# Five norms let the next stage's first pair of blocks start on unnormalised rows; masked key halves are left out

## The reference

```python
# first block, l = 0 (even) and 1 (odd)
x = x + even_mixer(rmsnorm(x, norm_mix[0]), ...)      # "f": gmlp gate and causal attention with forgetting
x = x + odd_mixer(rmsnorm(x, norm_mix[1]), ...)       # "o": differential attention and short convolution
x = x + memory_cross_attention(rmsnorm(x, norm_mem_q[l]), rmsnorm(mem, norm_mem_kv[l]), ...)   # "m0", "m1"
h = rmsnorm(x, norm_ffn[l]); x = x + swiglu(h, ...)   # l = 0: "ffn0";  l = 1: a mixture of 8 experts
# second block, l = 0, 1
sh1, sc1, g1, sh2, sc2, g2 = split(silu(c) @ ada_w[l] + ada_b[l], 6)
x = x + g1 * hybrid_mixer(rms_norm(x, norm1_w[l]) * (1 + sc1) + sh1, ...)      # "b0", "b1"
x = x + g2 * conv_ffn(rms_norm(x, norm2_w[l]) * (1 + sc2) + sh2, ...)          # "ffn1", "ffn2"
```

## Time and profile before

| | us |
|---|---|
| runs of the kernel before | 2389.85, 2386.93, 2387.54 |
| median | 2387.54 |
| profiled execution | 2386.44 |
| its span from the first to the last instruction | 2384.6 |
| mean granted clock of TensorE | 0.993 |

### The profile page before, as it was taken

How to read it: one execution, slowest core, us unless ns; L and a number is a source line. 1 busy time by engine, 2 the same in 40 slices (tenths; PEclk the granted TensorE clock), 3 DMA queues, 4 the chain that set the end, 5 groups by cost and what they waited for, 6 DMA issues and landing times.

```text
span 2384.6 us, 39695 instructions
## 1 busy us (share of the span) xinstructions
PE 2341.5 (98%) x14994; PEld 2125.4 (89%) x14994; DVE 1949.3 (82%) x2674; ACT 1522.7 (64%) x2078; POOL 0.8 (0%) x6
## 2 busy tenths in 40 slices
PE   8999999999999999999999999999999999999998
PEld 7999999899978888888888888887999999999998
DVE  6756877986689999999998989897887877886664
ACT  5655443545477887878787878786645554645552
POOL 0000000000000000000000000000000000000000
PEclk9999999999999999999999999999999999999999
DMA  9443779546579898999999999997323658323440
GB/s 378 154 165 142 283 289 350 236 158 267 203 260 375 336 373 338 371 345 362 347 362 346 364 351 360 358 354 306 142 106 142 247 220 329 143 107 141 181 156 19
DMA packets 88271, 623.67 MB, mean 262 GB/s; under 512 B 9764, under 2 KB 11464, under 8 KB 13384
## 3 DMA queue, kind: packets, MB, share of 16 engines
q1 hardware_dynamic: 87600, 621.26, 68.3%
q10 hardware_dynamic: 536, 0.53, 0.1%
HBM read 620.70 MB, written 1.05 MB: 261 GB/s over the span
## 4 chain that ended last, share of the span: by engine, by line
PE 90%; DVE 7%; ACT 2%; issue 1%; DMA 0%; SPq 0%; DVEq 0%; ACTq 0%
PE bank L654 14%; PE bank L656 14%; PE bank L655 14%; PE bank L674 10%; PE bank L678 10%; PE bank L675 10%; PE bank L875 3%; PE bank L874 3%; PE bank L872 3%; DVE ring_r L1745 2%; PE bank L1076 1%; PE bank L1087 1%; PE bank L1244 1%; DVE ring L1730 1%; PE bank L983 1%
## 5 line engine op out<-in xcount | busy, mean ns | idle before, releaser
L1745 DVE TENSOR_TENSOR ring_r<-ring,ring_r 128x1024 fp32r<-128x1024 f32 x402 | 489.5, 1222 | 182.0 <-ACT ring_r L1321 181.5
L1321 ACT ACTIVATE ring_r<-ring 128x1024 fp32r<-128x1024 f32 x402 | 423.0, 1055 | 299.6 <-PE bank L678 134.2
L674 PE MATMUL bank<-XH,ring_r 128*128 128x256 f32 x2000 | 493.0, 284 | 1.9 <-DVE ring_r L1745 1.9
L675 PE MATMUL bank<-XH,ring_r 128*128 128x256 f32 x2000 | 490.5, 283 | 0.0
L2213 DVE TENSOR_TENSOR ring_r<-ring,Z_r 128x1024 fp32r<-128x1024 f32 x336 | 408.4, 1224 | 34.8
L2213 DVE TENSOR_TENSOR ring_r<-ring,mhat_r 128x1024 fp32r<-128x1024 f32 x336 | 402.6, 1221 | 29.9 <-ACT mhat_r L1575 20.5
L1575 ACT ACTIVATE Z_r<-ring 128x1024 fp32r<-128x1024 f32 x336 | 356.7, 1062 | 92.0 <-PE bank L656 91.1
L1575 ACT ACTIVATE mhat_r<-ring 128x1024 fp32r<-128x1024 f32 x336 | 355.6, 1063 | 82.8 <-PE bank L656 81.0
L674 PEld LDWEIGHTS bank<-XH,ring_r 128*128 128x128 f32 x2000 | 383.7, 192 | 3.2 <-DVE ring_r L1745 2.7
L675 PEld LDWEIGHTS bank<-XH,ring_r 128*128 128x128 f32 x2000 | 383.8, 192 | 0.1
L655 PE MATMUL bank<-ring_r,xn_r 128*128 128x512 f32 x896 | 350.2, 391 | 0.0
(11 more groups left out here) (358 smaller groups left out, 3727.9 us busy)
## 6 DMA issues: line engine op xcount, KB each, us to landing
ring<-in_experts SPq DMA_DIRECT2D x336, 1024.0 KB, 6.9
ring<-in_stream SPq DMA_DIRECT2D x245, 1024.0 KB, 7.2
ring<-in_stream SPq DMA_DIRECT2D x8, 512.0 KB, 6.1
xT<-in_xT SPq DMA_DIRECT2D x2, 512.0 KB, 4.6
mhat<-in_memT SPq DMA_DIRECT2D x1, 1024.0 KB, 16.4
swap<-in_early SPq DMA_DIRECT2D x1, 1024.0 KB, 18.3
swap<-in_late SPq DMA_DIRECT2D x1, 1024.0 KB, 10.2
out_T<-xn SPq DMA_DIRECT2D x8, 128.0 KB, 2.0
```

Source lines behind the costliest of these rows:

```text
L674: pe.matmul(dst, hi[:, a], x_hi(kb), start=(n == 0), stop=False)
L675: pe.matmul(dst, lo[:, a], x_hi(kb), start=False, stop=False)
L1321: act.activation(wh(Q), raw(Q), ACT.Copy).then_inc(sems["whi"], 1)
L1745: dve.tensor_tensor(raw(Q, ring_r), raw(Q), wh(Q).bitcast(F32), ALU.subtract).then_inc(sems["wlo"], 1)
```

## The change

For norms 3, 4, 9, 10 and 11 (PLAIN):

- ACT writes x times the gain, unnormalised, as the high part (plain_high), DVE its low part (plain_low), in the residual loop before. PE runs the next stage's first pair of blocks from these (plain_blocks); norm_sums stands inside that pair after tile 5 (6 in norms 4 and 10) of the high products, norm_spread after tile 1 of the low ones. The filler is gone.
- All squares are added up on DVE (direct(i) is 0).
- ACT copies the spread values from PSUM to `roots` in SBUF. DVE multiplies from there, and also scales the first pair's results (scaled). With a shift, two further columns go with the first pair's rows, which give the shift's part of the result; it is added afterwards.
- The second pair, and all that follows, uses the normalised rows as before.
- low() calls are put in other places: after norm_column in each norm; in the o section three calls with rows=False, then low(1), low(2) in place of low(2, rows=False), low(4); modulation_done(0) comes behind o.k's copies; modulation_done(1) and the gain of norm 10 come before ffn1's residual loop.
- ACT's order at norm 10: prep(2) before the root; the evacuations of b1.hf 2 and 3, the shifts of 0 and 1, prep(2), and then the chain on z.

For the attentions f and o (CAUSAL): scores, bias adds, maxima, exponentials, transposes and products with v leave out the wholly masked half of the first query tile (seen, seen_rows); in f the score's four products have 128 columns for the first query tile.

```diff
-EXPOSED = (3, 4, 9, 10, 11)
...
 def direct(i):
-    return 2 if i in (4, 10, 12) else 1
+    return 0 if i in PLAIN else 2 if i == 12 else 1
...
+def plain_blocks(i, dsts, ws, one_bank=False):
+    n, width = PLAIN[i], S + 2 if i in SHIFT else S
+    def sums_between(kb):
+        if kb == (6 if i in (4, 10) else 5):
+            norm_sums(i)
+    def spread_between(kb):
+        if kb == 1:
+            norm_spread(i)
+    return two_blocks(dsts, ws,
+                      lambda kb: plain_hi[:, kb, 0:width], lambda kb: plain_lo[:, kb, 0:width],
+                      lambda kb: W(pe, "uh", n, kb + 1), lambda kb: W(pe, "ul", n, kb + 1), one_bank, sums_between, spread_between)
...
+def root_rows(i):
+    key = f"spread{i}"
+    G.wait_full(act, key)
+    G.drained(act.activation(roots, bank[G.bank(key)][:, 0:S], ACT.Copy), key)
...
 # ACT, a feed-forward stage
+    for kb in range(4, KB):
+        if 4 <= kb < 7:
+            prep()
+        squares(ni, kbs=[kb])
+        plain_high(ni, kb)
+    prep()
     root(ni)
+    root_rows(ni)
     split_x(ni, base)
-    prep()
...
 # DVE, a feed-forward stage
-    norm(ni)
+    norm_column(ni)
+    low(rows=False)
+    norm_apply(ni)
...
+    scaled(first_rows[:, 1, :], ni, f"ffn{i}.gu0", 0, 0 if i else S).then_inc(sems["fr"], 1)
     x_low(inst, base)
-    low(rows=False)
...
 # DVE, the o section
-norm(4)
-x_low("o")
-low(2, rows=False)
-dve.memset(BM[:, :, 0, P:S], NEG)
-low(4)
-modulation_done(0)
+low(1, rows=False)
+norm_column(4)
+low(1, rows=False)
+norm_apply(4)
+x_low("o", kbs=range(0, 4))
+low(1, rows=False)
+x_low("o", kbs=range(4, 8))
+for h in range(2):
+    G.wait_full(dve, "o.q", h)
+for h in range(2):
+    G.drained(scaled(fm(zs(0))[:, h, :], 4, "o.q", h, scale=float(CHUNK) ** -0.5), "o.q", h)
+low(1)
+low(2)
 for h in range(H):
     evac("o.k", h, fm(zs(1))[:, h, :])
     low()
+modulation_done(0)
...
 # ACT, b1
+for m in (2, 3):
+    evac("b1.hf", m, z[:, m * S:(m + 1) * S])
+for m in range(2):
+    W(act, "hz", 0, m + 1)
+    G.drained(act.activation(z[:, m * S:(m + 1) * S], z[:, m * S:(m + 1) * S], ACT.Identity,
+                             bias=shifts[:, 2 + m:3 + m]), "b1.hf", m)
+prep(2)
...
 # PE, f section
+n = (t + 1) * P
+dst = seen(b[:, t * S:(t + 1) * S], t)
+pe.matmul(dst, q4[:, h, t * P:(t + 1) * P], k4[:, h, 0:n], start=True, stop=False)
```

More of the change, by code:

```diff
@@ L395, in build @@
                     release.append((f"{nm[:4]}.res", 3))
+                elif nm in ("ffn1.gu", "ffn2.gu") and j == 0 and q == 0:
+                    release.append((f"{nm[:4]}.g0", 0))
                 elif nm.endswith(".gu") and q % 2:
@@ L424, in plan_mem, with plan_ffn @@
                 G.at[f"m{l}.k", 4 + n] = G.at[f"m{l}.k4", n]
[L426 to L429, removed]
+        def plan_ffn(i, ni, res):
+            if i:
+                G.plan(f"ffn{i}.g0", 1, (G.bank(res, 0),))
+            first = G.bank(res, 1 if i else 0)
+            G.plan(f"ffn{i}.gu0", 1, (first,))
+            G.plan(f"nrm{ni}", 1, (G.bank(res, 4),))
+            G.plan(f"spread{ni}", 1, (G.bank(res, 5),))
+            G.turn[LO] = first + 1
+            G.plan(f"ffn{i}.gu0b", 1, LO)
+            G.at[f"ffn{i}.gu0", 1] = G.at[f"ffn{i}.gu0b", 0]
+            for j in range(1, FB // 2):
                 G.plan(f"ffn{i}.gu{j}", 2, LO)
@@ L704, in split_ready, with proj_f @@
                         lambda kb: W(pe, "xl", 0, low_base[inst] + order.index(kb) + 1))
-            def proj_f(nm, j, key, x_hi=xh, x_lo=xl, have=(ready, ready), order=range(KB), between=None, paired=False):
+            def proj_f(nm, j, key, x_hi=xh, x_lo=xl, have=(ready, ready), order=range(KB), between=None, paired=False, plain=None):
                 if paired:
@@ L774, in norm_sums @@
                 G.wait_free(pe, key)
-                if i in EXPOSED:
-                    keep_busy(key, 2)
                 W(pe, "sqa", i)
-                for n, kb in enumerate([0] + list(range(first, KB))):
+                rows = [0] + list(range(first, KB))
+                for n, kb in enumerate(rows):
                     if n:
@@ L1652, in _ @@
                 else:
-                    squares(10)
+                    for kb in range(KB):
+                        squares(10, kbs=[kb])
+                        plain_high(10, kb)
+                    prep(2)
                     root(10)
+                    root_rows(10)
                 split_x(8 + 2 * l, 48 * l)
@@ L1735, in modulation_done @@
             def modulation_done(l):
+                assert not [w for w in waiting if w[0] == l]
                 W(dve, "adar", l, NADA)
@@ L1778, in norm, with x_low @@
                 norm_apply(i, src, dst)
[L1780 to L1781 removed]
+            def x_low(inst, base=None, kbs=range(KB)):
+                for kb in kbs:
                     W(dve, "xh", SPLIT[inst], kb + 1)
@@ L2324, in _ @@
                 else:
-                    dlink(dve.tensor_scalar(gA, modc[:, o + 8:o + 16], 1.0, None, ALU.add))
-                    dlink(dve.tensor_tensor(gA, gA, col("norm1", 8 * l, 8), ALU.mult))
-                    norm(10)
-                    x_low("b1", o)
-                    low(6)
+                    low(1)
+                    norm_column(10)
+                    low(1)
+                    norm_apply(10)
+                    x_low("b1", o, range(0, 4))
+                    low(1)
+                    x_low("b1", o, range(4, 8))
+                    for m in range(2):
+                        G.wait_full(dve, "b1.hf", m)
+                        dve.tensor_copy(shifts[:, 2 + m:3 + m], bank[G.bank("b1.hf", m)][:, S:S + 1])
+                        scaled(fm(zs(5))[:, m, :], 10, "b1.hf", m).then_inc(sems["hz"], 1)
+                    low(3)
                 z, E, T9, T10, kk, hq = zs(5), zs(3), zs(9), zs(10), zs(8), zs(4)
```

287 lines of the change are left out of this document (205 added, 82 removed).

## The result

The changed kernel takes 2400.87 us (median of 5, 2400.14 to 2403.97) against 2387.8: a ratio of 1.0059, with an interval of 1.0048 to 1.0070. It is slower by 13.1 us. The forecast was slower by 5.2, and its range ended at 2397. The profiled execution took 2403.97 us, its span is 2402.2 and the mean granted clock is 0.987, where before had 0.993.

What follows compares the result with a forecast made beforehand. The prediction took PE (98% busy) to bound the kernel, with DVE (82%) making it wait. Its terms summed to +5.2 us: 2391.6 for the profiled execution, 2392.7 for the median, range 2384 to 2397.

Steps and rivals of the forecast that it cites:

- masked halves: f section: a quarter of the score columns goes, also fewer transposes and p.v products; -1.15 us, ends 0 and 3.05.
- norms 3, 9 and 11: PE's pause at these norms goes, DVE's list sets the fifth block's start; -1.9, -1.6 and -0.7 us.
- stream and norm 4: o section: SP waits for ada1,0's late last product, o.gc's weights queue behind; +8.2 us in place of -1.3, bounds 5.5 to 11.
- norm 10: ACT's chain starts 1.1 later and b1.rq waits 1.7 to 2.8, +1.1 us; a dropped clock there, +1.2 us.
- the +1.3 of the late norm_apply: Norm 4: busy DVE starts norm_apply later, by at most 1.3 us.
- the -2.6 of DVE's savings: Norm 4 and o section: DVE does less in row_max steps, mask fill, normalising and combining; -2.6 us in all.
- Rival B: Norms 3, 9 and 11 pay by PE's path, DVE keeping up: 3.6, 4.5 and 3.6 us gained, 2385.2; 12 in 100.
- Rival C: More dropped clocks at new pauses, at o.gc or inside a pair, 1.7 us each; two more make 2396; 20 in 100.
- the main one: The forecast's main case: the terms as summed, from 2389 to 2396 us; 51 in 100.
- Rival A: The weight stream at o.gc is not late and the result isn't slower: 2383.2 or 2381.9 us; 15 in 100.
- The rule on PSUM and SBUF sources: DVE products from copied roots: eight would be 0.5 us shorter, 2.6 over five norms, result 2390.1; 2 in 100.

Runs made afterwards that it cites:

- a3: The kernel before with only the masked halves left out, all norms in the old form: 2386.22 us, ratio 0.9990.
- c1: The changed kernel with norms 4 and 10 in the old form and section b1's PSUM banks planned as in the kernel before: 2383.09 us, ratio 0.9986.
- a1: The changed kernel with the third low() call at norm 4 again allowed to carry a modulation product: 2390.53 us, ratio 1.0012.
- a4: The changed kernel with norm 4 in the old form (filler, normalised first pair, products in the old places): 2389.22 us, ratio 1.0008.
- c4: a1 with section b1's PSUM banks set as far as norm 10's new form allows: 2387.18 us, ratio 0.9997.
- b3: a1 with filler products put where PE waits in norm 4's new form (five ahead of the sums, eight ahead of o.SA's last scores): 2390.18 us, ratio 1.0007.
- c3: The kernel before with five more filler products at norm 3, so that all behind is entered later: 2392.32 us, ratio 1.0018.
- b1: As a run, not the section: the changed kernel with norms 4 and 10 in the old form: 2385.78 us, ratio 0.9994.
- a2: The kernel before with norm 4's first low() call carrying no modulation product and modulation_done(0) behind o.k's copies: 2397.88 us, ratio 1.0049.

## Why the prediction was wrong, point by point

**What the 13.1 us are.** The terms of the forecast, and what differences of medians give for them:

| term | forecast | measured | from |
|---|---|---|---|
| masked halves | -1.15 | -1.5 | a3 |
| norms 3, 9 and 11 | -4.2 | -2.7 | c1's 4.2 less 1.5 |
| stream and norm 4 | +8.2 | +11.6 | 10.3 (after less a1) and 1.3 (a1 less a4) |
| norm 10 | +2.3 | +2.8 | c4 less c1 (4.1), less the 1.3 |
| banks of b1 | 0 | +3.35 | a1 less c4 |
| sum | +5.2 | +13.6 | |

The sum closes by its making, since each step starts where the last one ended; the 0.5 beyond 13.1 is the median of before, which moved from 2387.8 to 2387.2. Each line is good to about 2 us. Two steps of the prediction failed: the stream's term was too small by 3.4, and the banks of section b1 were put at nothing and cost 3.35. The norms' gains, 1.5 short, come third.

**The stream, +8.2: right in cause and place, too small.** The step that failed is the anchor in time. I let DVE reach the product 1.1 earlier, and subtracted the gains ahead of the section in terms of their own. In fact the section is entered 1.5 early, and DVE still comes to the product at 481.36, as late as before (481.23 in rows 7). So between norm 3 and the product DVE lost 1.6 where I had it gain 1.1: 2.7 of the miss. SP issued at 482.62, and ACT got its data at 495.07, 12.45 behind the issue against the 11.9 of the sum: the transfer was nearly right, 0.55 more. The low part stands at 496.16 against 486.17, 10.0 later. Counted from the entry the section costs 11.5, just outside the term's bounds of 5.5 to 11.

**Norm 4, -1.3 without the stream: not seen.** It costs 1.3 by medians, with 2 either way. I had the +1.3 of the late norm_apply and the -2.6 of DVE's savings, but not that PE waits 1.40 for the sums of squares and 2.23 at o.v, and runs at half clock behind both (423.5 to 426.9, and 452.27 above). It may be that o.v's slots come free later for this and DVE waits for ACT's preparations, but little of it shows: those waits are 5.6 us between 408 and 480 against 4.9 before. b3 shows that filler cures the clock and, in its place, most of the time; the end of the kernel doesn't see it.

**Norms 3, 9, 11, -1.9, -1.6, -0.7: right where they stand, not in the end.** The low parts behind them gained 2.1, 1.8 and 1.0 in a1, at the term's sizes. Rival B (PE's path alone) is refuted by the waits of 0.6 for DVE in each. But medians give 2.7 for 4.9. c1's column shows where it goes back: 5.7 are lost between the router and b0. a3 and c3 lose 2.6 and 2.5 there with the same 10.2 us at half clock in the router, so about 2.6 of the 5.7 is the clock. The other 3.1 is the wait at the end of the experts, 6.2 in c1 instead of 3.3. The same two stand in a4 and b1.

**Masked halves, -1.15 in f: 0.9** by the starts, and 1.9 more in o, which I had inside norm 4's -2.6. Net 1.5.

**Norm 10, +1.1 and +1.2: right.** PE waits 2.51 at b1.rq (I said 1.7 to 2.8), the section loses 2.3 by the table, and a stretch of 3.4 at half clock follows.

**The banks of section b1: a term that isn't in the sum.** I had taken the diff of the plan for bookkeeping, and did not work out which bank each group gets. The first level then waits 3.20 for DVE's mask of the last head instead of 1.6 for an earlier one, and a stretch at half clock follows: 3.35 by c4, 2.7 by c1.

**Rival C, 20 in 100, was the case besides the main one.** The changed kernel's profile has eleven stretches at half clock ahead of the last norm against six. The new pauses that C named, at o.gc and inside a pair (norm 4), are among them; the router, the banks and o.v, which it did not name, too. The forecast priced the clock only at norm 10. Rival A is refuted by a1 and a2.

Two places of the Trainium skill. The rule on PSUM and SBUF sources ("VectorE: DVE Perf Modes", The TRN2 errata) did not show: L1910 from the copied roots takes 3.26 and 3.25 us for eight at norms 4 and 10, as L1769 did from PSUM at norm 10 (3.22). On the clock, the Trainium skill ("TensorE: Matmul & The Clock Gate", What's actually happening) says that how many products run slowly varies with the gate's phase at the kernel's start. The runs of one kernel agree (below), and c3 goes further: 2.0 us put in within the kernel changed the time by 5.1.

## What to carry to other kernels

When calls that release a ring slot are moved, count the releases between each load's slot and its use, in the order of the queue that issues the loads: one call fewer in a group of eight cost 10 us here. Work out the bank plan after any insertion into a round-robin planner, for sections far behind the change as well. A pause filled with useless products is not waste to be saved: a run with the filler left out (10.9 us more here) prices it, before one prices what takes its place. And a gain seen in its place can be gone at the end, so follow it through the sections behind.

## What the runs showed of the hardware

The granted clock fell to half behind a pause of 1.40 us (422.66 in the changed kernel, half clock from 423.5 to 426.9). It also fell in the router section, where PE never stood still and its fp32 products are of 8 and 128 columns (648 to 652 before: busy 4.00 of 4.00, clock 0.67). That stretch was 3.4, 10.2 or 13.7 us long for the same products in the fourteen kernels. Within one kernel the slower runs are those of the lower mean clock: c1's eleven go from 2381.27 at 0.993 to 2386.73 at 0.990. A difference of 2 us between two versions of this kernel can be of this kind alone.

At the end of the experts' loop PE stood 3.28 us for DVE before. In the changed kernel's profile the same place shows 3.6 and in c1's 6.2 us put down to issue; in c1 DVE was through at 1655.2 and PE began at 1658.17. It is 6.3 in a4 and 6.9 in b1. What makes it longer was not found, and some 3 us of these three kernels' times hang on it.
